# Opening of a fused two-block kernel: ScalarE's work on weights and inputs in an even order, and unread products between TensorE's bias products

## The reference

```python
c_act = jax.nn.silu(c)
mod = jnp.dot(c_act, ada_w[l]) + ada_b[l]
sh1, sc1, g1, sh2, sc2, g2 = jnp.split(mod, N_MOD, axis=-1)
h = modulate(rms_norm(x, norm1_g[l]), sh1, sc1)          # h * (1 + scale) + shift
z = jnp.einsum('bsd,de->bse', h, w_in[l]) + b_in[l]
mq, mk, mv, mo, mi, mf, aq, ak, av, ga, gb = jnp.split(z, split_points, axis=-1)
...
qa = rope(split_heads(aq, A_HEADS, A_HEAD_DIM), positions)   # needs the sines and cosines of the positions
```

## Time and profile before

| | |
|---|---|
| time, median of 3 runs | 1390.16 us (1389.7, 1390.16, 1393.82) |
| profiled execution, first to last instruction (span) | 1388.5 us |
| PE busy | 1362.2 us, 98% |
| DVE, ACT, POOL busy | 1037.2, 887.4, 653.5 us |
| first weight product on PE | at 20.28 us |
| end of the opening's three blocks (next bias product) | at 57.66 us |

### The profile page before, as it was taken

How to read it: one execution, slowest core, us unless ns; L and a number is a source line. 1 busy time by engine, 2 the same in 40 slices (tenths; PEclk the granted TensorE clock), 3 DMA queues, 4 the chain that set the end, 5 groups by cost and what they waited for, 6 DMA issues and landing times.

```text
span 1388.5 us, 32152 instructions
## 1 busy us (share of the span) xinstructions
PE 1362.2 (98%) x9840; PEld 1267.2 (91%) x9840; DVE 1037.2 (75%) x2233; ACT 887.4 (64%) x1861; POOL 653.5 (47%) x503
## 2 busy tenths in 40 slices
PE   7999999999999999999999999999999999999998
PEld 4798999999999989999999999999998888888886
DVE  6778867888988496439999868888876666666665
ACT  5668765555446665547888687777765555555554
POOL 4896783000006868688888887777730000000000
PEclk9999999999999999999999999999999999999998
DMA  9776565988983633565555554444455666566662
GB/s 343 272 253 228 198 244 189 323 320 317 336 331 122 215 127 123 188 216 168 182 182 183 182 168 154 159 156 151 154 166 194 195 192 189 194 196 193 189 194 90
DMA packets 79798, 283.84 MB, mean 204 GB/s; under 512 B 8822, under 2 KB 8950, under 8 KB 79611
## 3 DMA queue, kind: packets, MB, share of 16 engines
q1 hardware_dynamic: 79738, 283.07, 59.7%
HBM read 281.99 MB, written 1.05 MB: 204 GB/s over the span
## 4 chain that ended last, share of the span: by engine, by line
PE 79%; POOL 6%; issue 5%; PEld 3%; DVE 3%; ACT 2%; DMA 1%; PEldq 0%; POOLq 0%; SPq 0%; DVEq 0%
PE psA L1821 19%; PE psA L1825 19%; PE psA L1824 19%; POOL w_lo L563 6%; PE psD L1821 6%; PE psD L1824 5%; PE psD L1825 5%; PE psD L2283 1%; PEld psA L1821 1%; PE psD L2284 1%; PEld psA L1825 1%; PEld psA L1824 1%; DMA xT<-x 1%; DVE arena L1540 1%; PEld psD L2240 0%
## 5 line engine op out<-in xcount | busy, mean ns | idle before, releaser
L628 ACT CAST w_hi<-raw 128x512 fp32r<-128x512 f32 x864 | 529.5, 620 | 424.7 <-PE psA L1821 306.8
L563 POOL TENSOR_TENSOR w_lo<-raw,w_hi 128x512 fp32r<-128x512 f32 x476 | 632.7, 1348 | 353.6 <-ACT w_hi L628 343.1
L1821 PE MATMUL psA<-h_hi,w_hi 128*128 128x256 f32 x1568 | 452.8, 289 | 0.7 <-POOL w_lo L563 0.5
L1824 PE MATMUL psA<-h_lo,w_hi 128*128 128x256 f32 x1568 | 443.0, 283 | 0.0
L1825 PE MATMUL psA<-h_hi,w_lo 128*128 128x256 f32 x1568 | 442.9, 282 | 0.0
L1099 DVE TENSOR_TENSOR w_lo<-raw,w_hi 128x512 fp32r<-128x512 f32 x388 | 266.1, 691 | 152.7 <-ACT w_hi L628 151.6
L1821 PEld LDWEIGHTS psA<-h_hi,w_hi 128*128 128x128 f32 x1568 | 300.0, 191 | 4.3 <-issue 1.5
L1824 PEld LDWEIGHTS psA<-h_lo,w_hi 128*128 128x128 f32 x1568 | 300.2, 191 | 0.1
L1825 PEld LDWEIGHTS psA<-h_hi,w_lo 128*128 128x128 f32 x1568 | 299.9, 191 | 0.0
L1821 PE MATMUL psA<-w_hi,u_hi 128*128 128x512 f32 x512 | 199.4, 389 | 0.4 <-DVE u_lo L1162 0.4
L1825 PE MATMUL psA<-w_hi,u_lo 128*128 128x512 f32 x512 | 199.2, 389 | 0.0
(11 more groups left out here) (391 smaller groups left out, 2212.5 us busy)
## 6 DMA issues: line engine op xcount, KB each, us to landing
raw<-expert_down SPq DMA_DIRECT2D x128, 512.0 KB, 3.2
raw<-expert_up SPq DMA_DIRECT2D x128, 512.0 KB, 4.2
arena<-ada SPq DMA_DIRECT2D x96, 512.0 KB, 5.3
raw<-gateup SPq DMA_DIRECT2D x44, 512.0 KB, 5.4
raw<-feat SPq DMA_DIRECT2D x28, 512.0 KB, 3.8
raw<-win SPq DMA_DIRECT2D x24, 512.0 KB, 3.3
raw<-down SPq DMA_DIRECT2D x22, 512.0 KB, 6.1
raw<-wout SPq DMA_DIRECT2D x20, 512.0 KB, 3.2
```

The costliest lines, as they stand in the source:

```text
L563: nc.gpsimd.tensor_tensor(w_lo[:, s * HALF:(s + 1) * HALF], raw_half(n), w_hi[:, s * HALF:(s + 1) * HALF].bitcast(F32), ALU.subtract).then ...
L628: nc.scalar.copy(w_hi[:, n % SLOTS * HALF:(n % SLOTS + 1) * HALF], raw_half(n)).then_inc(hi_ready, 1)
L1821: first = mm(o, w[0], m[0], start=start, stop=False, skip_group_check=True)
L1824: mm(o, w[0], m[1], start=False, stop=False, skip_group_check=True)
```

## The change

On ACT, the order becomes: two halves, `first_h(0)`, and then three halves between each chunk and the next; behind `first_h(7)` come the sine and one last half. The work is the same: 24 halves, eight chunks, one sine with one table load.

On PE, five unread products go between the bias products of block 2 and the sum of squares, and eight between the bias products of block 0 and those of block 1. They go to bank 3 of psD, which the bias product of block 1 then starts anew. No other wait is added.

```diff
             act.wait_ge(sem("scale_b"), 1)
-            for j in range(0, KC, 2):
-                split(1)
+            split(1)
+            for j in range(KC):
                 first_h(j)
-                split(1)
-                first_h(j + 1)
-                split(1)
-                if j == 2:
-                    act.wait_ge(sem("angles"), 1)
-                    nc.scalar.activation(trig[:, 0:2, :, :], trig[:, 0:2, :, :], ACT.Sin).then_inc(sem("trig"), 1)
+                if j < KC - 1:
+                    for _ in range(3):
+                        split_half()
+            act.wait_ge(sem("angles"), 1)
+            nc.scalar.activation(trig[:, 0:2, :, :], trig[:, 0:2, :, :], ACT.Sin).then_inc(sem("trig"), 1)
+            split_half()
             act.wait_ge(ada_used, 2 * KC)
...
             banks = [[tok_bank(A, 2) for _ in range(NT)]]
+            keep_clock(psD[:, BANKS - 1, :], 5)
             pe.wait_ge(sem("x_sums"), 1)
             Dr.full(mm(ssq_bank[:, 0:T], ones[:, :], xn[:, 0, :], start=True, stop=True))
-            banks = [[tok_bank(Dr, 0) for _ in range(NT)], [tok_bank(Dr, 1) for _ in range(NT)]] + banks
+            first_block = [tok_bank(Dr, 0) for _ in range(NT)]
+            keep_clock(psD[:, BANKS - 1, :], 8)
+            banks = [first_block, [tok_bank(Dr, 1) for _ in range(NT)]] + banks
```

## The result

The changed kernel takes 1393.78 us (median of 19 runs, 1390.23 to 1397.7), the kernel before 1391.83 us beside it (median of 19, 1389.5 to 1393.82). The ratio is 1.0015, 95% interval 1.0008 to 1.0022: slower by 0.15%, 2.1 us. That is inside the 0.3% that the prediction took as no change, but on the other side than the forecast of -0.5 us, and the median lies above the range. A part of the miss in the absolute number is the base: 1390.16 was the median of three runs, and 19 give 1.7 us more; counted from that base, the range would have reached 1394.1. So it is the direction that was missed, more than the size. The ratios in this document are those on record with their intervals; they are not the quotients of the medians printed beside them, which differ from them by up to 0.001.

What follows compares the result with a forecast made beforehand. PE, busy 98% of the span, was taken as the bound. Chunk 7 at 52.53 + 4.21 products + 0.33 late sine + 0.08 = 57.15 against 57.66: -0.5 us, so 1389.7 us; range 1387.7 to 1392.4.

Steps and rivals of the forecast that it cites:

- the even order: ACT's three halves between chunks: a wait for h_lo at every chunk from 1, 4.57 us a chunk against 4.10 of PE work.
- The five and the eight products: PE's unread products before the weight products: at most 0.22 us an instruction, the eight hidden in the wait for h_lo.
- a rise at around 16 us: PE's clock goes up during the eight products, so weight products run at 0.228 us from the start; 2.2 us at most.
- The rival without a rise: Clock stays low until the weight products: PE starts them at 21.16, opening ends at 59.24, +1.6 us, 1391.7; chance 0.22.
- the sum: The prediction's added-up timeline of the opening, ending with the bias product behind the loop at 57.15 against 57.66 us.
- The cover of 0.4 us: DVE turns to the reciprocal 0.4 us after the root ends, covering the 0.06 delay of the sum of squares.
- the late sine: Sine and its table load before ACT's last half: PE waits 0.22 at chunk 7's last half, 0.33 us with the restart.
- the rival in which it meets POOL in every chunk: h_lo runs while POOL is busy in every chunk: 6 x 0.26 more, +1.1 us, 1391.2; chance 0.12.
- the drain of the Trainium skill: Rival: about 1.38 us added to the sine's table load, about +0.8 us or 1391.0 in all; chance 0.03.
- What lies further back: Behind the opening: no change forecast; only the range's low end took half of the 3.30 us at the lower clock.
- the theory: Stated before the experiments: even order costs, unread products cost when holding PE beyond h_lo, the clock's rise decides little.

Runs made afterwards that it cites:

- even order alone: Kernel before with only ACT's new order and the sine behind chunk 7, no unread products: ratio 1.0011, 1392.44 against 1389.94 us.
- products alone: Kernel before with only PE's five and eight unread products, ACT's order unchanged: ratio 1.0005, 1391.99 against 1389.94 us.
- three instead of eight: Changed kernel with three unread products, not eight, between the bias products of blocks 0 and 1: ratio to the kernel before 1.0015, 1392.63 us.
- moved order: Kernel before with ACT doing two halves, chunk 0, two halves, chunk 1, then three between chunks; no unread products: ratio 0.9984, run again 0.9981.
- products in time, order before: Kernel before with block 0's bias products ahead of the sum of squares, eight unread products behind it; ACT's order unchanged: 0.9999, 1391.9 us.
- products in time, moved order: Moved order with block 0's bias products ahead of the sum of squares and eight unread products behind it: ratio to the kernel before 0.9987, 1389.62 us.
- products to first weight product: Moved order, block 0's bias products ahead of the sum of squares, eight products with zeros after all bias products: ratio to kernel before 0.9990, 1389.76 us.

## Why the prediction was wrong

The step that failed is the one that hid the unread products: it left the first weight product at 20.28, 7.46 behind the input's sum, as in the kernel before. Measured are 9.35 and 9.44. What the even order costs from chunk 1 on was forecast right. Step by step, in the order of the prediction:

- *The five and the eight products.* Wrong, and with it the first weight product. I priced an instruction at 0.22 at most; with a gap at each change of kind they took 0.23 to 0.26, 2.62 and 3.72 us in the first profile. Alone that is 0.6. The heavier error is the condition: I took a rise at around 16 us, and where it did not come, PE arrived at 22.58 instead of 20.28. The rival without a rise gave 21.16 and an end at 59.24; measured were 22.58 and 60.81. Of the 1.42 us at the start, 0.35 are the later sum of squares (the input's lateness, not the products), 0.20 the eight products, the rest the gaps at each change of kind (the sum of squares alone took 1.16, 13.71 to 14.87, where the sum has 0.86). The cover of 0.4 us for the sum of squares came from one execution with a late input. It held in the first profile of the changed kernel, where the input was later still. In the other three profiles with the five products the input's sum begins between 11.56 and 11.75, and they held the sum of squares until 13.35 to 13.44, 1.2 to 1.3 longer than its 0.48.
- *The rise of the clock.* It varies with the execution, 22.4 to 25.4 in the kernel before and 19.8 to 25.6 in the changed one. The Trainium skill (TensorE: Matmul & The Clock Gate, Part 1: The HAM clock gate) says that it varies between runs of one kernel, and the rows agree. In the execution with an early rise the opening still ended at 57.95, not at 57.15 as the sum has it, because PE came at 21.10 and not at 20.28. A rise at 16 us did not occur in any profile with this order of PE, so what it would give is not shown.
- *The even order.* Right: 4.57 for a chunk was forecast, 4.60 measured, with a wait at every chunk from 1 on. From chunk 1 to the end of the loop the sum has 32.30; measured are 32.24 and 32.25, against 30.80 and 30.82 before. So the even order with the late sine costs 1.4 us in both executions.
- *h_lo.* 0.43 in the loop, so the rival in which it meets POOL in every chunk fell.
- *The late sine.* Forecast 0.33 with the restart, measured 0.19 and 0.11 (59.22 against 58.80 + 0.23, and 0.50 against 0.39). The load is followed by the sine after 0.02 us; the drain of the Trainium skill (ScalarE: Activation LUTs, What ACT_TABLE_LOAD costs) is not seen here either.
- *What lies further back.* I let it stand unchanged.

The table splits each profile into consecutive parts: the start of the input's sum, from there to the first weight product (what the products hold), chunk 0 (above all how long the lower clock lasts), from chunk 1 to the bias product behind the loop (what the order costs), and from there to the end of the span.

| execution | input's sum | to first weight product | chunk 0 | chunk 1 to end of loop | loop ends | the rest | lower stretch near 425 us |
|---|---|---|---|---|---|---|---|
| before, first | 12.82 | 7.46 | 6.58 | 30.80 | 57.66 | 1330.8 | short |
| before, second | 11.68 | 7.45 | 5.75 | 30.82 | 55.70 | 1333.7 | long |
| changed, first | 13.23 | 9.35 | 5.99 | 32.24 | 60.81 | 1333.8 | long |
| changed, second | 11.66 | 9.44 | 4.60 | 32.25 | 57.95 | 1332.3 | short |
| even order alone | 13.00 | 7.45 | 6.07 | 32.25 | 58.77 | 1332.3 | long |
| products alone | 11.56 | 10.49 | 5.88 | 30.79 | 58.72 | 1331.3 | short |
| three instead of eight | 11.75 | 8.43 | 7.03 | 32.15 | 59.36 | 1334.0 | long |
| moved order, first | 12.60 | 7.46 | 5.57 | 28.65 | 54.28 | 1332.1 | short |
| moved order, second | 11.89 | 7.45 | 5.95 | 28.65 | 53.94 | 1331.9 | short |
| products in time, order before | 11.75 | 8.04 | 5.75 | 30.81 | 56.35 | 1334.1 | long |
| products in time, moved order | 11.67 | 8.06 | 5.68 | 28.65 | 54.06 | 1332.6 | short |
| products to first weight product | 12.33 | 7.44 | 4.30 | 31.29 | 55.36 | 1331.6 | short |

What the order costs is the same in every profile with that order and the sine at the same place (30.8, 32.2, 28.65), so it belongs to the kernel; only the last row departs, by the three waits told above. What the products hold depends on the execution too: with the same program on PE it is 9.35 with a late input, 9.44 with an early input and an early rise, and 10.49 with an early input and a late rise. The input, chunk 0 and the rest vary from execution to execution. Chunk 0 alone lies between 4.30 and 7.03, so the theory was wrong where it said that the rise decides little. For the changed kernel the products cost 1.9 to 2.0 and the order 1.4; chunk 0 gives back 0.9 in the mean of two profiles each. That is 2.5 us, against 2.1 from the runs with an interval of 1.1 to 3.1.

Of the 6.1 us between the two spans first seen, 3.15 were made in the opening (0.41 of them by the input) and 2.95 behind it. The rest varies just as much in the kernel before (1330.8 and 1333.7), and the length of the lower stretch alone does not explain it (1332.3 stands beside a long and a short one). So nothing here shows that the change costs anything further back.

A case that depends on the execution should have been a mean over several: the input's arrival and the rise were both taken from one profile, and the chance of 0.22 for the case without a rise before the weight products was too low.

Left open: what the products give or cost by themselves in the mean. Their interval reaches from -0.0008 to +0.0018, and the runs of the changed kernel lie up to 7.5 us apart. The one profile of them alone gives more (3.0 at the start, with 0.3 back in chunk 0), but it is one execution, with an early input and a late rise.

## What to carry to other kernels

Where a producer is held by the progress of its consumer, what counts is which slot of the ring the producer's side work stands behind, not how evenly it is spread: moving each chunk one half forward turned +0.0011 into -0.0016, and 32.25 from chunk 1 on into 28.65 (0.3 of it by the sine, which was moved too). Products that only keep the clock up can lose twice. In the changed kernel they delayed what they were to speed up; where they ended before the wait, the clock was down again when it was wanted; in the one profile where they ran up to the first weight product the clock stayed up, and another wait took the gain. And what fits into a wait in one profile need not fit in the next: a single profile of a 0.1% question is one draw, so take two of each kernel, and measure each part from the event that starts it, here the input's sum, before explaining a difference.

## Hardware behaviour not expected

- A clock that rose at 16.3, under eight unread products, was back at the lower level at 19.7, with four bias products of four rows and a wait of 1.73 us between (the first kernel with products that end in time); in the second it was up at 16.0 and down at 19.4.
- The stretch at the lower clock near 425 us was 3.4 us long in some executions and 6.8 in others, of both kernels.
- The input's sum began anywhere between 11.56 and 13.23 us in executions of kernels in which DVE does the same up to there.
- An h_lo that starts beside a running operation of POOL ends 0.28 behind the end of that operation, where that is later than its usual 0.43: 0.93 long in the moved order (40.51), 1.22 and 1.29 in the kernel with products up to the first weight product (so in all 25 cases of the twelve profiles).
